# Decode attention: recent keys and values in the upper half of TensorE's array, and a first gelu on ScalarE

## The reference, cut to what matters

```python
# compressed: 63 windows of 32 past tokens, through gelu(hid) @ w2
o_c = softmax(q . ck) @ cv
# selected: blocks of 64 past tokens, 16 of 17 kept, and the new token
o_s = softmax(q . k_s) @ v_s
# recent (window): the last 512 tokens, the oldest out, the new one in
o_w = softmax(q . kwin) @ vwin
o = g[..., 0:1] * o_c + g[..., 1:2] * o_s + g[..., 2:3] * o_w
```

## Time and profile before

| | |
|---|---|
| time, median of 3 runs | 2225.27 us (2223.93 to 2228.70) |
| profiled execution, span on the core | 2256.8 us (its own time beside the span was not recorded) |
| TensorE / VectorE / ScalarE / GpSimd busy | 1674.6 / 1388.1 / 308.4 / 720.4 us |
| decode stage, first instruction to the merge's first product | 470.87 to 649.10 us |
| mean granted TensorE clock | 0.783 |

### The profile page before, as it was taken

How to read it: one execution, slowest core, us unless ns; L and a number is a source line. 1 busy time by engine, 2 the same in 40 slices (tenths; PEclk the granted TensorE clock), 3 DMA queues, 4 the chain that set the end, 5 groups by cost and what they waited for, 6 DMA issues and landing times.

```text
span 2256.8 us, 22422 instructions
## 1 busy us (share of the span) xinstructions
PE 1674.6 (74%) x7668; PEld 782.0 (35%) x7668; DVE 1388.1 (62%) x3457; ACT 308.4 (14%) x707; POOL 720.4 (32%) x883
## 2 busy tenths in 40 slices
PE   6997889976798928888877777566655666665666
PEld 5455776643385804554413443001000111110110
DVE  5999326521321646887455767985889644777544
ACT  3001224321201202221011110000000000000000
POOL 5910200043101653232333333333333333333331
PEclk9998879987999958999977888566566655566565
DMA  3111900044343359999999999999999999999997
GB/s 134 58 38 42 274 2 1 1 143 129 114 146 115 103 200 420 412 416 411 413 416 411 398 394 414 376 376 414 420 413 407 421 413 413 413 410 408 414 415 291
DMA packets 129901, 654.93 MB, mean 290 GB/s; under 512 B 22092, under 2 KB 37116, under 8 KB 59964
## 3 DMA queue, kind: packets, MB, share of 16 engines
q0 software_dynamic: 80000, 562.07, 61.8%
q1 hardware_dynamic: 49788, 91.42, 11.7%
HBM read 646.34 MB, written 11.26 MB: 291 GB/s over the span
## 4 chain that ended last, share of the span: by engine, by line
DMA 27%; PE 14%; DVE 12%; issue 7%; POOL 3%; ACT 0%; DVEq 0%; POOLq 0%; ACTq 0%
DMA ex_uv<-in_peer_uv,idxT 27%; PE ex_acc L2225 7%; DVE ex_uv L2347 5%; POOL ex_uv L2013 3%; PE ex_hb L2128 3%; PE ex_late L2150 1%; DVE ch_ci L1670 1%; DVE ch_sc L1667 1%; PE ex_late L2178 1%; DVE ch_iu L1670 1%; DVE ch_work L1704 1%; DVE ch_work L1707 1%; DVE ch_pick L1708 1%; DVE ch_work L1674 1%; PE ex_late L2198 1%
## 5 line engine op out<-in xcount | busy, mean ns | idle before, releaser
L2347 DVE SCALAR_TENSOR_TENSOR ex_uv<-ex_uv,ex_hb 128x1024 f32<-128x1024 f32 x520 | 628.5, 1220 | 430.7 <-DMA ex_uv<-in_peer_uv,idxT 335.9
L2013 POOL DMA_INDIRECT ex_uv<-in_peer_uv,idxT x520 | 494.4, 951 | 921.4 <-PE ex_acc L2225 798.7
L2128 PE MATMUL ex_hb<-ex_h_rows,spread 24*128 24x512 bf16 x1040 | 345.8, 493 | 429.0 <-DVE ex_uv L2347 405.1
L2225 PE MATMUL ex_acc<-ex_uv,wts 128*32 128x512 f32 x2080 | 414.8, 940 | 1.8 <-DVE wts L2263 1.8
L2128 PEld LDWEIGHTS ex_hb<-ex_h_rows,spread 24*128 24x128 bf16 x1040 | 52.7, 99 | 756.5 <-DVE ex_uv L2347 600.4
L2466 ACT ACTIVATE ex_gelu<-ex_dots 128x4 f32<-128x4 f32 x130 | 26.7, 205 | 1131.3 <-DVE ex_uv L2347 1101.8
L2225 PEld LDWEIGHTS ex_acc<-ex_uv,wts 128*32 128x32 f32 x2080 | 71.8, 146 | 244.9 <-issue 240.6
L1147 POOL MEMSET de_qbd<- 128x576 f32 x1 | 0.6, 579 | 203.8 <-POOLq L99 203.8
L2198 PE MATMUL ex_late<-hx,ex_ring 128*128 128x264 f32 x256 | 65.6, 413 | 0.0
L1838 PE MATMUL ro_pq<-hT,w_q 128*128 128x256 f32 x256 | 60.2, 390 | 1.6 <-POOL idxT L1763 1.6
L2198 PEld LDWEIGHTS ex_late<-hx,ex_ring 128*128 128x128 f32 x256 | 50.4, 202 | 16.9 <-issue 7.8
(11 more groups left out here) (487 smaller groups left out, 2405.3 us busy)
## 6 DMA issues: line engine op xcount, KB each, us to landing
ex_ring<-in_late_w SPq DMA_DIRECT2D x24, 1024.0 KB
gate_ring<-in_w_in SPq DMA_DIRECT2D x6, 2048.0 KB, 9.0
ex_uv<-in_peer_uv,idxT POOLq DMA_INDIRECT x520
w_q<-in_peer_w_q SPq DMA_DIRECT2D x8, 1024.0 KB, 8.0
w_out<-in_w_out SPq DMA_DIRECT2D x2, 2048.0 KB, 18.1
ex_h_rows<-h_split SPq DMA_DIRECT2D x65, 48.0 KB
pr_x<-in_x_prompt SPq DMA_DIRECT2D x4, 512.0 KB, 4.8
gate_ring<-in_w_in_heads SPq DMA_DIRECT2D x1, 2048.0 KB
```

What stands on the lines that cost most here:

```text
L2013: pool.indirect_dma_start(uv[:, s % SLOTS].rearrange("p j n -> p (j n)"), None, table, bass.IndirectOffsetOnAxis(ap=S.idxT[:, t:t + 1], ax ...
L2128: last = pe.matmul(hb[s % 2][:, CHUNK * h:CHUNK * h + CHUNK], spread[p, k % LOAD, :], h_rows[p, l % 2, CHUNK * h:CHUNK * h + CHUNK], start ...
L2225: last = pe.matmul(acc[LANE * g:LANE * g + LANE, CHUNK * h:CHUNK * h + CHUNK], wts[:, s % (2 * BATCH), LANE - 1 - r:2 * LANE - 1 - r], uv[ ...
L2347: dve.scalar_tensor_tensor(out=rows_, in0=rows_, scalar=1.0, in1=hb[s % 2][:], op0=ALU.mult, op1=ALU.mult, accum_out=dots[:, B % 2, c:c + ...
```

## The change

The recent keys and values are computed in the upper 64 columns of the array, so that their rows lie in partitions 64 to 127 beside those of the selected keys:
- `swin`, `s_win`, the recent half of the statistics (`stw`), of `anew`, `wgt` and `od` move to partitions 64 to 127; `seq`, `grp` and `grow` are loaded for both halves (3 more loads, the count of `consts` goes from 5 to 8).
- `key_scores` issues selected, recent, selected.
- the products with the selected and recent values are interleaved (a recent one behind every second selected one), behind one wait for both sets of probabilities.
- VectorE weighs the recent output ahead of the selected one; `od` has two halves, added by a product with `stack` (two identities on top of each other, made by VectorE as its first operation) in place of the transpose.
- the two transposes of `anew` become one.
- ScalarE's first operation is a gelu on one column.

```diff
-        seq = sb("seq", [ROWS, NB])
-        grp = sb("grp", [ROWS, NKV])
-        grow = sb("grow", [ROWS, 3])
+        seq = sb("seq", [P, NB])
+        grp = sb("grp", [P, NKV])
+        grow = sb("grow", [P, 3])
+        stack = sb("stack", [P, ROWS])
+        warm = sb("warm", [P, 1])
+        lower, upper = slice(0, ROWS), slice(ROWS, P)
...
@@ sync
-            for m, name in ((touch, "c_touch"), (same, "c_same"), (seq, "c_seq"), (grp, "c_group")):
+            for m, name in ((touch, "c_touch"), (same, "c_same")):
                 sp.dma_start(m[:], io[name]).then_inc(E["consts"], 16)
+            for rows_ in (lower, upper):
+                for m, name in ((seq, "c_seq"), (grp, "c_group")):
+                    sp.dma_start(m[rows_], io[name]).then_inc(E["consts"], 16)
             sp.wait_ge(E["g_saved"], 16)
-            sp.dma_start(grow[:], scratch.rearrange("b (h j) -> (b h) j", j=3)).then_inc(E["consts"], 16)
+            for rows_ in (lower, upper):
+                sp.dma_start(grow[rows_], scratch.rearrange("b (h j) -> (b h) j", j=3)).then_inc(E["consts"], 16)
@@ scalar
+            act.activation(warm[:], S.hbias[:, 0:1], ACT.Gelu_apprx_tanh)
...
-            act.activation(s_win, s_win, ACT.Exp, bias=st[:, 4:5], accum_out=st[:, 5:6]).then_inc(E["win_exp"], 1)
+            act.activation(s_win, s_win, ACT.Exp, bias=stw[:, 4:5], accum_out=stw[:, 5:6]).then_inc(E["win_exp"], 1)
@@ vector
             dve.wait_ge(E["zeroed"], 3)
+            dve.tensor_tensor(stack[:], S.ident[:, 0:ROWS], S.ident[:, ROWS:P], ALU.add).then_inc(E["stacked"], 1)
...
-                dve.tensor_scalar(anew[:, j, :], seq[:], p, None, ALU.mult).then_inc(E["an_ready"], 1)
+                dve.tensor_scalar(anew[rows_], seq[rows_], p, None, ALU.mult).then_inc(E["an_ready"], 1)
...
-            for j, (done, bank) in enumerate((("oc_done", po[0:ROWS, 1, 0:KVW]), ("os_done", ph[0:ROWS, 128:128 + KVW]),
-                                              ("ow_done", swin[:, 0:KVW]))):
+            for j, (done, rows_, bank) in enumerate((("oc_done", lower, po[lower, 1, 0:KVW]),
+                                                     ("ow_done", upper, swin[upper, 0:KVW]),
+                                                     ("os_done", lower, ph[lower, 128:128 + KVW]))):
                 dve.wait_ge(E[done], 1)
+                n = (0, 2, 1)[j]
                 for g in range(NKV):
                     half = bank[:, HD * g:HD * g + HD]
-                    if j == 0 and g == 0:
-                        link(dve.tensor_scalar(od[:], half, wgt[:, 0, 0:1], None, ALU.mult))
+                    if j < 2 and g == 0:
+                        link(dve.tensor_scalar(od[rows_], half, wgt[rows_, n, 0:1], None, ALU.mult))
...
-                        if j == 2 and g == 1:
+                        if j and g == 1:
                             ins.then_inc(E["od_ready"], 1)
@@ tensor, key_scores
-                for j in range(2):
-                    pe.matmul(ssel[:, j, :], qbd[:, ROWS * b:ROWS * b + ROWS], kT[:, b % 2, 512 * j:512 * j + 512],
-                              start=(b == 0), stop=(b == NB - 1))
-                pe.matmul(swin[:], qbd[:, ROWS * b:ROWS * b + ROWS], kT[:, b % 2, PAST:PAST + WB],
-                          start=(b == 0), stop=(b == NB - 1)).then_inc(E["ds_done"], 1)
+                q_of = qbd[:, ROWS * b:ROWS * b + ROWS]
+                pe.matmul(ssel[:, 0, :], q_of, kT[:, b % 2, 0:512], start=(b == 0), stop=(b == NB - 1))
+                pe.matmul(swin[upper], q_of, kT[:, b % 2, PAST:PAST + WB], start=(b == 0), stop=(b == NB - 1))
+                pe.matmul(ssel[:, 1, :], q_of, kT[:, b % 2, 512:PAST], start=(b == 0),
+                          stop=(b == NB - 1)).then_inc(E["ds_done"], 1)
@@ tensor, tail
-            for j in range(2):
-                last = pe.transpose(ph[0:NB, ROWS * j:ROWS * j + ROWS], anew[:, j, :], S.ident[0:ROWS, 0:ROWS])
-            last.then_inc(E["anT_done"], 1)
+            pe.transpose(ph[0:NB, 0:P], anew[:], S.ident[:]).then_inc(E["anT_done"], 1)
             pe.wait_ge(E["anT_kept"], 1)
...
-            for n, (done, bank, probs, vals, new, chunks) in enumerate((
-                    ("os_done", ph[0:ROWS, 128:128 + KVW], psm, vsel, S.vs, NPG),
-                    ("ow_done", swin[:, 0:KVW], pwm, vwin, S.vw, WT))):
-                pe.wait_ge(E["pt_kept"], n + 1)
-                for b in range(NB):
-                    for c in range(chunks):
-                        pe.matmul(bank, probs[:, c, ROWS * b:ROWS * b + ROWS], vals[:, b, c, :],
+            pe.wait_ge(E["pt_kept"], 2)
+            o_sel, o_win = ph[lower, 128:128 + KVW], swin[upper, 0:KVW]
+            for b in range(NB):
+                for c in range(NPG):
+                    pe.matmul(o_sel, psm[:, c, ROWS * b:ROWS * b + ROWS], vsel[:, b, c, :],
+                              start=(b == 0 and c == 0), stop=False)
+                    if c % 2 == 0:
+                        pe.matmul(o_win, pwm[:, c // 2, ROWS * b:ROWS * b + ROWS], vwin[:, b, c // 2, :],
                                   start=(b == 0 and c == 0), stop=False)
-                pe.matmul(bank, anT[:, n, :], new[:], start=False, stop=True).then_inc(E[done], 1)
-            pe.wait_ge(E["od_ready"], 1)
-            pe.transpose(tp[0:HD, 0, 0:ROWS], od[:], S.ident[0:ROWS, 0:ROWS]).then_inc(E["odT_done"], 1)
+            pe.matmul(o_win, anT[:, 1, :], S.vw[:], start=False, stop=True).then_inc(E["ow_done"], 1)
+            pe.matmul(o_sel, anT[:, 0, :], S.vs[:], start=False, stop=True).then_inc(E["os_done"], 1)
+            pe.wait_ge(E["stacked"], 1)
+            pe.wait_ge(E["od_ready"], 2)
+            pe.matmul(tp[0:HD, 0, 0:ROWS], od[:], stack[:], start=True, stop=True).then_inc(E["odT_done"], 1)
```

More of the change, by code:

```diff
@@ L1107, in stage_decode @@
         drop = sb("drop", [ROWS, 16])
-        st = sb("st", [ROWS, 16])
-        s_win = kT[:].rearrange("p b n -> p (b n)")[0:ROWS, 0:WB + 1]
-        junk = sb("junk_d", [ROWS, NB])
-        anew = sb("anew", [ROWS, 2, NB])
+        both = sb("st", [P, 16])
+        st, stw = both[lower], both[upper]
+        s_win = kT[:].rearrange("p b n -> p (b n)")[upper, 0:WB + 1]
+        junk = sb("junk_d", [P, NB])
+        anew = sb("anew", [P, NB])
         anT = sb("anT", [NB, 2, ROWS])
-        wgt = sb("wgt", [ROWS, 3, NKV])
-        od = sb("od", [ROWS, HD])
+        wgt = sb("wgt", [P, 3, NKV])
+        od = sb("od", [P, HD])
         taps_of = xT[:].rearrange("p b g (s c) -> p b g s c", s=CMP_STRIDE // 2)
@@ L1126, in stage_decode @@
         ssel = ps("dssel", [ROWS, 2, 512])
-        swin = ps("dswin", [ROWS, 512])
+        swin = ps("dswin", [P, 512])
         names = ("consts", "zeroed", "wlanded", "imp_read", "tr_done", "kept0", "kept1", "hid_done", "gh_ready",
@@ L1296, in _ @@
                                    drop[:].unsqueeze(2).broadcast_to([ROWS, 16, SEL_BLOCK]), ALU.add))
-            for j, to in enumerate((s_sel[:, PAST:PAST + 1], s_win[:, WB:WB + 1])):
-                link(dve.scalar_tensor_tensor(out=junk[:], in0=po[0:ROWS, 0, NB * j:NB * j + NB], scalar=1.0, in1=seq[:],
-                                              op0=ALU.mult, op1=ALU.mult, accum_out=to))
+            for j, (rows_, to) in enumerate(((lower, s_sel[:, PAST:PAST + 1]), (upper, s_win[:, WB:WB + 1]))):
+                link(dve.scalar_tensor_tensor(out=junk[rows_], in0=po[rows_, 0, NB * j:NB * j + NB], scalar=1.0,
+                                              in1=seq[rows_], op0=ALU.mult, op1=ALU.mult, accum_out=to))
             link(dve.tensor_reduce(st[:, 2:3], s_sel, AX_X, ALU.max))
             dve.tensor_scalar(st[:, 2:3], st[:, 2:3], -1.0, None, ALU.mult).then_inc(E["sel_max"], 1)
-            link(copy(s_win[:, 0:WB], swin[:]))
+            link(copy(s_win[:, 0:WB], swin[upper]))
             link(dve.memset(s_win[:, 0:1], NEG))
-            link(dve.tensor_reduce(st[:, 4:5], s_win, AX_X, ALU.max))
-            dve.tensor_scalar(st[:, 4:5], st[:, 4:5], -1.0, None, ALU.mult).then_inc(E["win_max"], 1)
-            for j, (done, p) in enumerate((("sel_exp", s_sel[:, PAST:PAST + 1]), ("win_exp", s_win[:, WB:WB + 1]))):
+            link(dve.tensor_reduce(stw[:, 4:5], s_win, AX_X, ALU.max))
+            dve.tensor_scalar(stw[:, 4:5], stw[:, 4:5], -1.0, None, ALU.mult).then_inc(E["win_max"], 1)
+            for rows_, done, p in ((lower, "sel_exp", s_sel[:, PAST:PAST + 1]), (upper, "win_exp", s_win[:, WB:WB + 1])):
                 dve.wait_ge(E[done], 1)
-                dve.tensor_scalar(anew[:, j, :], seq[:], p, None, ALU.mult).then_inc(E["an_ready"], 1)
+                dve.tensor_scalar(anew[rows_], seq[rows_], p, None, ALU.mult).then_inc(E["an_ready"], 1)
             dve.wait_ge(E["room"], 1)
@@ L1411, in _ @@
             last.then_inc(E["sc_done"], 1)
-            for j in range(2):
-                last = pe.matmul(po[0:ROWS, 0, NB * j:NB * j + NB], qall[:], S.kTs[:, j, :], start=True, stop=True)
```

(8 more changed lines are left out.)

18 lines of the change are left out of this document (9 added, 9 removed).

## The result

Measured in turn on one chip, the kernel before takes 2226.98 us (median of 4 runs, 2223.93 to 2231.22), the changed one 2213.89 us (4 runs, 2209.69 to 2216.51). The ratio is 0.9937, with a 95% interval of [0.992, 0.9954]: 13 us or 0.6% faster. Forecast were 2211.6 us and a sum of -13.7 us. The profiled execution of after has a span of 2214.7 us and a time of 2216.47.

What follows compares the result with a forecast made beforehand. Waits in the expert stage bound the kernel, but decode savings reach the end one for one. Terms -6.9 - 7.5 + 0.5 + 0.1 - 0.1 + 0.2 = -13.7 us take 2225.3 to 2211.6; 8-in-10 range 2202 to 2218.

Steps and rivals of the forecast that it cites:

- Scores: Decode's loop over eight sequences: two recent passes hide beside four selected ones, 0.87 us per sequence, -6.9 us.
- Values: Decode's products with the values: recent passes, spread between selected ones, are all hidden in the other half, -7.5 us.
- (b): Values' products: short 128-column passes overlap by half only, so 7.5 becomes 3.7 us, time 2215.4; chance 0.10.
- (c): Scores and values: one half's weight loads hold up the other, giving back 7.1 and 1.7 us, 2220.4; chance 0.03.
- (d): Scores and values: each change of halves empties the array, 0.16 us at 80 places, 2238.8 us; chance 0.03.
- Tail: Behind the values' products: four VectorE operations follow the last product, +0.5 us, and a two-pass final product, +0.1.
- added wait of part 2: Before the values' products: waiting for both sets of turned probabilities costs nothing to 0.1 us, taken as 0.
- Start: Decode's start: VectorE's added sum ahead of the query copies delays the first transposes, +0.2 us; extra loads cost 0.
- The early gelu: Decode's start on ScalarE: moving the table load there costs nothing and gains 0, with -7 us as other bound.
- (a): Decode's first gelu: the table load causes its late start, so removing it saves 6.4 us more, 2205.2; chance 0.28.
- the stall belongs to the gathers and stays: Decode's first gelu: the page gathers cause its 6.4 us late start, so it remains and the gain is 0.
- the test that I set myself: Decode's first instruction to the merge's first product: 178.2 us becomes 164.5; wrong if it shrinks by 18 or more.

Runs made afterwards that it cites:

- 9: Changed kernel with the recent keys' product back in the lower 64 columns, its order kept: 2219.21 us, ratio 0.9973 to the kernel before.
- 7: Changed kernel with scores in the old order (selected, selected, recent), recent still in the upper columns: 2213.6 us, ratio 0.9933 to the kernel before.
- 6: Changed kernel with all selected values' products first, then the recent ones, still in two halves: 2219.54 us, ratio 0.9969 to the kernel before.
- 4: Changed kernel with the recent values' products, closing one included, over all 128 columns: 2265.02 us, ratio 1.0068 to the kernel before.
- 3: Kernel before with only the early one-column gelu added as ScalarE's first operation: 2252.44 us, ratio 0.9995 to the kernel before.
- 11: Changed kernel without the early gelu, on a chip without late starts: 2213.45 us, ratio 0.9946 to the kernel before.
- 1: Kernel before, unchanged, run and profiled again: 2254.44 us, ratio 1.0005 to the kernel before.
- 12: Kernel before, unchanged, a third time, on a fourth chip: 2258.42 us, ratio 1.0025 to the kernel before.
- 5: Changed kernel, unedited, on a chip where the kernel before takes 2227.33 us: 2212.89 us, ratio 0.9936.
- 2: Changed kernel without the early gelu, on a chip where the kernel before takes 2253.5 us: 2248.77 us, ratio 0.9973.
- 10: Changed kernel with the recent keys' product over 128 columns, half of them zero: 2225.96 us, ratio 1.0004 to the kernel before.

## Why the prediction was right, and where not

**Scores** (-6.9): right to 0.1. 1.90 us per sequence, 6.86 in the loop, and 9 gives it back. The reason given, two halves at once, holds; the order of the change, on which I said nothing, is not needed (7).

**Values** (-7.5): right in mechanism, as 6 shows by taking the alternation away. The doubt about 128-column passes (b) falls: 0.073 us a pass at full clock, two thirds of 0.108. Measured is -7.8, of which 0.3 is the clock's shorter half, inside the 2 us that I had kept for it.

**Weight loads** (c): fall with the same row; the loads of both halves lie under the passes.

**The slower rival** (d): a drain exists, at 0.17 us, close to the 0.18 from which it would decide. But it goes with the width, not with the half. The kernel never changes width inside these loops, so the rival did not happen; 4 is the kernel in which it does, and it is slower than before.

**Tail**: forecast +0.5 and +0.1, measured +0.80. The last operation on `od` ends 1.34 us behind the products (604.69 to 606.03), outside the 0.6 to 1.2 that I gave as a sign. The added wait of part 2 and the single transpose, forecast 0 to 0.1 and -0.1: the stretch that holds them grew by 0.25. The wait cost nothing, and the single transpose saved nothing: the way over it is 0.09 longer. Start: +0.2, measured 0.14. Sum -13.7, measured -13.5 by the rows and 13 by the runs.

**The early gelu** (0): right, and (a) is refuted by 3 and 11. One of my reasons was misread. The copy at 489.07 isn't that of the transposes of 483.46; VectorE copies these, and ScalarE takes the next ones:

```profile
486.25 0.69 DVE L1247 COPY de_xT<-dtp 128x512 f32<-128x512 f32 x1 [4.26 <-remote]
...
486.99 0.72 PE L1357 MATMUL dtp<-ident,nat 128*128 128x128 f32 x4 [2.90 <-DVE de_xT L1247]
```

So in place of one stall of 5.0 us with no load near there are two, of 2.2 on VectorE (484.09 to 486.25) and 1.4 on ScalarE (487.71 to 489.07). The reason stands with the smaller sizes.

But the step read "the stall belongs to the gathers and stays", and "stays" failed: in the profile of after it isn't there. Late starts are there in all five profiles from chips on which before takes 2253 us (1 to 4, 12) and in the first profile of before, and in none of the eight others (after, 5 to 11). I had the sign of this in hand: the first profile's span was 31.5 us above the median of the runs. I carried that difference over as if it lay evenly over everything. It most likely lay largely in stalls that those timed runs don't have. For the same reason the test that I set myself, that I am wrong if decode shrinks by 18 us or more, fired (34.6) with the forecast right: it compared an execution with the stalls and one without, not two kernels. On equal terms (1 and 2) decode shrinks by 13.4. That the time came out so near to 2211.6 is in part luck: the comparison ran where before takes 2227 us. On the other kind of chip the nearest relation of the changed kernel (2) took only 4.8 us less by its median.

**Open:** what makes TensorE's counts come up to 8.4 us behind the modelled ends of its products on some chips while pages are gathered. At the largest late start of each of five profiles (before, 1, 2, 3, 12) the trace has the count, and the engine starts 0.02 to 0.03 us behind it; some smaller ones have no count in the trace. The changed kernel as it stands was never profiled on such a chip, nor the kernel before on one without; that the whole 14 us reach the end there rests on 2, whose median gives 5 and whose profile 12.

## What to carry to other kernels

Products that use only half of the array's columns can be put in the other half: two streams then run in the time of the longer, if passes for the two are within a few of each other in the program. This was seen for fp32 products over all 128 rows with 128 and 512 columns of moving data. Don't let short products over half and over all columns alternate: each change cost 0.17 us, more than a pass of 0.108. Before a stall in a profile is put into a sum, compare that profile's time with the timed runs: a profile far above them shows waits that they may not have.

## What the runs showed of the hardware

- TensorE starts a pass for a free half of the columns ahead of up to three passes that stand before it in the program (6, 7); its count to other engines still came in program order (7: 579.76, where its own passes end at 578.91 and the last earlier one at 579.73).
- A change between products over 64 and over 128 columns costs 0.17 us (4, 10). In the one profile with the values in such an alternation (4) the granted clock also stayed at half for some 15 us of busy work, where the same stretch without it comes back after 4.6 (after). That the alternation did this isn't shown: in 10 the scores alternate at full clock.
- The same kernel takes 2225 to 2227 us on two chips and 2253 to 2254 on two others, with copies and gelus up to 8.5 us late under the gathers on the latter only. At the largest of these it is TensorE's count that comes late, measured from the modelled end of its products (3: end 503.33, count 511.77, copies at 511.79).
